# Unread products in TensorE's waits, pooling's copies and gates on ScalarE, and a third first tile four blocks behind

## The reference

```python
def _modulate(x, gain, shift, scale):
    return _rmsnorm(x, gain) * (1 + scale) + shift
...
def _pool_mixer(h, w_in, w_grp, scale, w_out):
    z = (h @ w_in).astype(jnp.float32).reshape(bsz, length, POOL_GROUPS, POOL_GROUP_DIM)
...
    pooled = (cs[:, hi, gidx] - cs[:, lo, gidx]) / cnt - z
    y = jnp.einsum('blgc,gcd->blgd', pooled, w_grp.astype(jnp.float32)).reshape(bsz, length, POOL_WIDTH)
    y = (y * scale.astype(jnp.float32)).astype(h.dtype)
    return y @ w_out
```

## Time and profile before

| | us |
|---|---|
| median of 3 runs | 1941.17 (1937.13 to 1942.27) |
| profiled execution, its time | 1939.76 |
| its span, first to last instruction | 1937.9 |
| PE busy | 1886.3 (97%) |
| DVE busy | 1535.0 (79%) |
| ACT busy | 920.9 (48%) |
| POOL busy | 400.0 (21%) |
| mean granted TensorE clock | 0.987 |

### The profile page before, as it was taken

The page is one execution under the profiler, slowest core; times in us unless marked ns, Lnnn a source line. Parts: engine busy times, 40 slices in busy tenths (PEclk is TensorE's granted clock), DMA queues, the critical chain, the costliest instruction groups (busy, mean ns, idle before and its releaser), DMA issues.

```text
span 1937.9 us, 38299 instructions
## 1 busy us (share of the span) xinstructions
PE 1886.3 (97%) x13216; PEld 1690.2 (87%) x13216; DVE 1535.0 (79%) x2617; ACT 920.9 (48%) x1476; POOL 400.0 (21%) x205
## 2 busy tenths in 40 slices
PE   5999999999999999999999899999999999999998
PEld 5999999999888888888888899999888888888887
DVE  6876589957998888888886669994889888886554
ACT  3464444544555544445444444454545544444544
POOL 1544468820000000000002347880000000000000
PEclk9999999999999999999998999999999999999999
DMA  8855345556655555578882345555664555555553
GB/s 319 321 198 195 132 164 180 182 181 207 211 168 173 174 173 173 173 268 318 323 309 95 118 147 173 180 176 183 217 209 160 173 174 173 173 173 187 193 194 130
DMA packets 104181, 376.42 MB, mean 194 GB/s; under 512 B 12464, under 2 KB 12464, under 8 KB 103856
## 3 DMA queue, kind: packets, MB, share of 16 engines
q1 hardware_dynamic: 103680, 373.43, 56.8%
q0 software_dynamic: 432, 2.10, 0.3%
HBM read 374.43 MB, written 1.05 MB: 194 GB/s over the span
## 4 chain that ended last, share of the span: by engine, by line
PE 55%; issue 19%; POOL 15%; DMA 4%; DVE 4%; ACT 2%; SPq 1%; POOLq 0%; DVEq 0%; ACTq 0%
PE O L1480 12%; PE O L1482 11%; PE O L1481 11%; POOL wL L405 9%; PE ring L1446 8%; POOL wL L392 6%; PE ring L1448 4%; DMA raw<-in_u 3%; PE ring L1232 2%; PE ring L1233 2%; PE ring L1234 2%; PE ring L1422 2%; DVE wL L673 2%; ACT wH L434 1%; PE O L1422 1%
## 5 line engine op out<-in xcount | busy, mean ns | idle before, releaser
L434 ACT ACTIVATE wH<-raw 128x1024 fp32r<-128x1024 f32 x608 | 644.8, 1061 | 921.6 <-DMA raw<-in_v 370.6
L673 DVE TENSOR_TENSOR wL<-raw,wH 128x1024 fp32r<-128x1024 f32 x416 | 509.2, 1224 | 234.8 <-ACT wH L434 229.9
L1232 PE MATMUL ring<-hX,wH 128*128 128x256 f32 x1512 | 434.5, 287 | 8.0 <-DVE wL L661 5.7
L1233 PE MATMUL ring<-hX,wH 128*128 128x256 f32 x1512 | 429.0, 284 | 0.0
L1234 PE MATMUL ring<-hX,wL 128*128 128x256 f32 x1512 | 428.8, 284 | 0.0
L1480 PE MATMUL O<-wH,gateH 128*128 128x512 f32 x1024 | 406.0, 396 | 0.3 <-DVE wL L673 0.3
L1482 PE MATMUL O<-wH,gateL 128*128 128x512 f32 x1024 | 400.2, 391 | 0.0
L1481 PE MATMUL O<-wL,gateH 128*128 128x512 f32 x1024 | 399.0, 390 | 0.0
L1446 PE MATMUL ring<-hX,wH 128*128 128x512 f32 x1024 | 367.3, 401 | 0.0
L1232 PEld LDWEIGHTS ring<-hX,wH 128*128 128x128 f32 x1512 | 291.2, 193 | 10.5 <-ACT UV L541 4.0
L1233 PEld LDWEIGHTS ring<-hX,wH 128*128 128x128 f32 x1512 | 291.3, 193 | 0.1
(11 more groups left out here) (171 smaller groups left out, 2174.0 us busy)
## 6 DMA issues: line engine op xcount, KB each, us to landing
raw<-in_u SPq DMA_DIRECT2D x256, 512.0 KB, 3.4
raw<-in_v SPq DMA_DIRECT2D x256, 512.0 KB, 3.5
ada_v<-in_ada SPq DMA_DIRECT2D x40, 512.0 KB, 4.8
raw<-in_w_in SPq DMA_DIRECT2D x32, 512.0 KB, 4.8
raw<-in_w_q SPq DMA_DIRECT2D x32, 512.0 KB, 3.5
ada_s<-in_ada SPq DMA_DIRECT2D x20, 512.0 KB, 5.3
ada_f<-in_ada SPq DMA_DIRECT2D x16, 512.0 KB, 10.7
raw<-in_w_out SPq DMA_DIRECT2D x16, 512.0 KB, 3.4
```

Source lines behind the costliest of these rows:

```text
L434: nc.scalar.activation(wH[s % RAW][:, :], raw[s % RAW][:, :], ACT.Copy).then_inc(s_h, 1)
L673: nc.vector.tensor_tensor(wL[s % RAW][:, :], raw[s % RAW][:, :], wH[s % RAW][:, :].bitcast(fp32), ALU.subtract).then_inc(s_low, 1)
L1232: mm(bank[:, 0:T], a, xH[:, k0 + k, :], start=(first and k == 0), stop=False)
L1233: mm(bank[:, 0:T], a, xL[:, k0 + k, :], start=False, stop=False)
```

## The change

It has six parts.

1. `keep_clock(n, bank)` puts n fp32 matmuls of 128 x 128 into PE's queue whose results nobody reads: 12, 11, 2 and 4 of them around the first norm's work, one behind each of the last four mixing tiles, 3 + 3 + 5 around the norms 1 and 3, 4 in front of the transposes that end layer 0, 3 + 5 around norm 2, 3 in front of the last spread. 70 in all.
2. `first_tiles` waits only for `hH` before the two products with it, takes the product with `hL` behind them, and runs the third tile four blocks behind the first two.
3. The modulations of 16 and 24 matmuls in `w_u` and `p_in` are taken in lots of eight between tiles.
4. The split of w_out's tile 3 on ACT and the low half of its tile 2 on DVE are issued a few operations earlier.
5. In the pool stage ACT copies the products into `Z` and rounds the scaled group product straight from PSUM to `gH`; DVE makes `gL` from PSUM; `UV` holds no full gates there. Two of the eight group results go into `ring` banks.
6. The sums of a pair of tiles are taken one pair later on DVE.

```diff
--- before.py
+++ after.py
@@ -256,7 +256,7 @@
         def pool_bank(n):
-            return O[n % 4]
+            return (O[0], O[1], O[2], O[3], ring[2], ring[3], O[0], O[1])[n]
@@ ACT, layer 0 @@
                     for f in range(10, SGU_FT):
+                        if f == 14:
+                            ahead(W_OUT, 0, 0)
                         gated_high(f, f + 1)
                     act.wait_ge(s_small, SMALL)
-                    warm_root()
                     for j in range(KT):
                         for kk in range(2):
-                            ahead(W_OUT, j // 2, 2 * (j % 2) + kk)
+                            if j or kk:
+                                ahead(W_OUT, j // 2, 2 * (j % 2) + kk)
+                            if j == 0 and kk:
+                                warm_root()
@@ ACT, layer 1 @@
+                    def pooled_high(n):
+
+                        act.wait_ge(s_pg, n + 1)
+                        f = POOL_ORDER[n]
+                        nc.scalar.activation(gH[:, n, :], pool_bank(n)[:, 0:T], ACT.Copy, scale=ps[:, f:f + 1])\
+                            .then_inc(s_gH, 1)
+
                     for j in range(KT):
                         ahead(base, j // 4, j % 4)
+                        act.wait_ge(s_pe, base + j + 1)
+                        nc.scalar.activation(Z[:, POOL_ORDER[j], PAD:PAD + T], ring[j % 4][:, 0:T], ACT.Copy)\
+                            .then_inc(s_bank_v, 1)
+                        if j > 5:
+                            pooled_high(2 * (j - 6))
+                            pooled_high(2 * (j - 6) + 1)
+                    for n in range(4, KT):
+                        pooled_high(n)
                     warm_root()
-                    for f in range(KT):
-                        gated_high(f, SGU_FT + f + 1)
@@ DVE, layer 0 @@
                     for f in range(12, SGU_FT):
+                        if f == 13:
+                            ahead(W_OUT, 0, 0)
                         gated_low(f)
@@ DVE, layer 1 @@
-                    def pooled_full(n):
-
-                        dve.wait_ge(s_pg, n + 1)
-                        nc.vector.tensor_scalar(UV[:, SGU_FT + n, :], pool_bank(n)[:, 0:T],
-                                                ps[:, POOL_ORDER[n]:POOL_ORDER[n] + 1], None, ALU.mult).then_inc(s_gf, 1)
-
                     def pooled_low(n):
+
                         dve.wait_ge(s_gH, SGU_FT + n + 1)
-                        nc.vector.tensor_tensor(gL[:, n, :], UV[:, SGU_FT + n, :], gH[:, n, :].bitcast(fp32),
-                                                ALU.subtract).then_inc(s_gL, 1)
...
+                        f = POOL_ORDER[n]
+                        nc.vector.scalar_tensor_tensor(gL[:, n, :], pool_bank(n)[:, 0:T], ps[:, f:f + 1],
+                                                       gH[:, n, :].bitcast(fp32), ALU.mult, ALU.subtract).then_inc(s_gL, 1)
...
-                        nc.vector.tensor_copy(Z[:, f, PAD:PAD + T], ring[j % 4][:, 0:T]).then_inc(s_bank_v, 1)
...
+                    for j in range(1, KT):
+                        ahead(base, j // 4, j % 4)
+                        if j == 4:
+                            modulations(7, (8, 9, 10), O[3], (3,))
+                        if j in (3, 5, 7):
+                            pool(j - 2)
+                    pooled_low(0)
+                    pooled_low(1)
+                    pool(KT - 1)
+                    for n in range(2, KT):
+                        pooled_low(n)
@@ PE, first_tiles @@
+                for k in range(KT):
+                    if k % 4 == 0:
+                        weights(k // 4, 2)
+                    pe.wait_ge(s_hH, KT * n + k + 1)
+                    for t in range(2):
+                        high(t, k)
+                    if count > 2 and k > 3:
+                        if k == 4:
+                            weights(0, 3)
+                        high(2, k - 4)
+                        low(2, k - 4)
                     pe.wait_ge(s_hin, KT * n + k + 1)
...
+                    for t in range(2):
+                        low(t, k)
+                if count > 2:
+                    weights(1, 3)
+                    for k in range(4, KT):
+                        high(2, k)
+                        low(2, k)
@@ PE @@
+            def keep_clock(n, bank=None):
+
+                for _ in range(n):
+                    mm((ring[3] if bank is None else bank)[:, 0:P], mean_w[:, :], ident[:, :], start=True, stop=True)
+
@@ PE, group_product @@
-                if n >= 4:
-                    pe.wait_ge(s_gf, SGU_FT + n - 3)
+                if n in (4, 5):
+                    pe.wait_ge(s_bank_v, 4 + KT + n + 3)
+                if n > 5:
+                    pe.wait_ge(s_gL, SGU_FT + n - 5)
@@ PE, start @@
             pe.wait_ge(s_const, 6)
+            pe.wait_ge(s_acc, 4)
+            keep_clock(12)
             modulations(acc_f, 0, 1, KT, O[3])
             for j in range(KT):
                 mean(0, j)
+            keep_clock(6)
+            pe.wait_ge(s_acc, ADA_FRONT - 3)
+            keep_clock(5)
             spread(0)
+            keep_clock(2)
             modulations(acc_f, 1, 2, ADA_FRONT, O[3][:, KT:])
+            keep_clock(4)
@@ PE, layer 0 @@
-                            modulations(acc_s, 0, 2, ADA_FRONT + 2 * KT, O[3])
+                            modulations(acc_s, 0, 1, ADA_FRONT + 2 * KT, O[3], signal=False)
                         if t == 10:
+                            modulations(acc_s, 1, 2, ADA_FRONT + 2 * KT, O[3][:, KT:])
...
+                    pe.wait_ge(s_bank_a, 4 + 16 + 14)
                     for f in range(12, SGU_FT):
                         mix_tile(f)
+                        keep_clock(1, ring[1])
@@ PE, layer 1 @@
-                        if j == 3:
-                            modulations(acc_v, 2, 5, ADA_U1, O[3])
-                        if j == 4:
+                        if j < 5:
+                            modulations(acc_v, j, j + 1, ADA_U1, O[3][:, KT * (j - 2):], signal=(j == 4))
+                        if j == 5:
                             pe.wait_ge(s_late, 48)
-                        if j > 3 and j % 2 == 0:
-                            group_product(j - 4)
-                            group_product(j - 3)
+                        if j in (5, 6):
+                            group_product(2 * (j - 5))
+                            group_product(2 * (j - 5) + 1)
@@ PE, second and fourth norm @@
                 mean(n, KT - 2)
+                keep_clock(3, ring[1])
                 mean(n, KT - 1)
+                keep_clock(3)
                 spread(n)
+                keep_clock(5)
@@ PE, end of a layer @@
                 if layer == 0:
                     pe.wait_ge(s_mod, 6)
+                    keep_clock(4, ring[3])
...
+                keep_clock(3)
                 spread(2 * layer + 2)
+                if layer == 0:
+                    keep_clock(5)
```

More of the change, by code:

```diff
@@ L869, in _ @@
                         for s in range(2):
-                            ahead(W_OUT, j // 2, 2 * (j % 2) + s)
+                            if j or s:
+                                ahead(W_OUT, j // 2, 2 * (j % 2) + s)
                             if 2 * j + s - 1 in ADA_W_OUT:
@@ L918, in _ @@
                         pooled = vtok[:, 0, 2 * g * T:(2 * g + 2) * T].rearrange("p (c t) -> p c t", c=2)
-                        after(steps[0])
                         after(step(nc.vector.tensor_tensor(pooled, lev[cur][:, :, PAD:PAD + T],
@@ L1237, in first_tiles, with high, low, weights @@
             def first_tiles(base, n, emptied, before, count):
+                def high(t, k):
+                    mm(ring[t][:, 0:T], wH[t][:, k * P:k * P + P], hH[:, k, :], start=(k == 0), stop=False)
+                    mm(ring[t][:, 0:T], wL[t][:, k * P:k * P + P], hH[:, k, :], start=False, stop=False)
+                def low(t, k):
+                    ins = mm(ring[t][:, 0:T], wH[t][:, k * P:k * P + P], hL[:, k, :], start=False, stop=(k == KT - 1))
+                    if k == KT - 1:
+                        ins.then_inc(s_pe, 1)
+                def weights(half, tiles):
+                    if n == 0:
+                        pe.wait_ge((s_first_l, s_first_r)[half], 2)
+                    else:
+                        pe.wait_ge((s_l0, s_l1)[half], base - HALVES[base >= BASE["p_in", 1]] + tiles)
                 for t in range(count):
@@ L1241, in first_tiles @@
                 for k in range(KT):
-                    if k % 4 == 0 and n == 0:
-                        pe.wait_ge((s_first_l, s_first_r)[k // 4], 2)
-                    elif k % 4 == 0:
-                        pe.wait_ge((s_l0, s_l1)[k // 4], base - HALVES[base >= BASE["p_in", 1]] + count)
-                    pe.wait_ge(s_hin, KT * n + k + 1)
-                    for t in range(count):
-                        a, b = wH[t][:, k * P:k * P + P], wL[t][:, k * P:k * P + P]
```

(15 more changed lines are left out.)

28 lines of the change are left out of this document (5 added, 23 removed).

## The result

| | before | after |
|---|---|---|
| median, range | 1941.17 us (1935.34 to 1943.88, 5 runs) | 1926.24 us (1922.91 to 1928.93, 5 runs) |
| span of the profiled execution | 1937.9 us | 1924.4 us |
| mean granted clock | 0.987 | 0.992 |

The ratio is 0.9923, 95% interval 0.9904 to 0.9941: the change is faster by 0.8%. The forecast was 1924.5.

The account below looks back on a forecast made before the run. TensorE, busy in nearly every slice, was taken as the bound, through idle stretches, lower clock and queued work. Terms summing to 16.7 us gave 1923.1 us for the profiled execution, 1924.5 for the median; range 1917 to 1932.

Parts of the forecast that it names:

- rival 3: Pool stage: ACT becomes the bound, its copies wait behind splits and the stage gains nothing; 1930 us, chance 0.06.
- rival 4: A later stage takes the gain back through loads or POOL's low halves; 4 us left, 1937 us, chance 0.04.
- rival 5: Slower: the filled waits are no waits, what PE awaits hangs on its own queue; 1955 us, chance 0.03.
- rival 1: The upper clock level holds in every filled wait; gain 24.0 us, 1917.2 us, chance 0.12.
- rival 2: Clock falls at all norms anyway, unread products run low, partly on the path; gain 10.5 us, 1930.7 us, chance 0.20.
- (A): Start of the kernel: high products begin earlier and the first 48 products end sooner; gain 3.0 us.
- (C): First w_out tile: DVE's low half begins earlier, the third tile's wait is filled, the clock holds; gain 2.5 us.
- (D): Second norm and w_q: earlier load chain and upper clock, less unread products on the path; gain 2.4 us.
- (F): Pool stage: work moved from DVE to ACT, UV wait and low clock gone; gain 5.5 us, the largest term.
- (E): End of layer 0 and third norm: unread products delay the transposes 0.6 us, clock rises earlier; gain 0.3 us.
- (G): Fourth norm: 1.4 us from the earlier load chain and 0.4 from the clock; gain 1.8 us.
- (B): Modulations in w_u split into two lots with full products between, so the clock does not fall; gain 1.6 us.

Follow-up runs that it names:

- the second execution: The unaltered changed kernel measured again on another chip, beside the follow-up runs, with its own profile: 1925.21 us, ratio 0.9927 to the kernel before.

## Why the prediction was right, and where it wasn't

The time was right to 1.7 us, and rivals 3, 4 and 5 fell. ACT is busy 12.4 of 30.2 us in the pool stage and none of PE's longer waits there is for it, the u and v stages gave back only 0.3, and the unread products alone gain. Rivals 1 and 2 were each right somewhere: the level held for the first tiles behind all three norms, but the means and unread products of the second and fourth still ran into a low stretch. But the sum was right because errors of both signs met: (A), (C), (D) and (F) came 5.9 us short of their forecasts, and (E), (G) and the rest with (H) 3.2 above. That part is luck. Between the two profiles 13.5 of the 16.7 us came; between the medians, 14.9.

- **(A), 3.0 forecast, 0.2 measured.** The step that failed is that the eleven unread products before the spread cost nothing. I had priced only the two behind it (up to 0.6), and my sum has no term for the eleven. They are 22 records at 0.215 us at the lower level, 4.7 us, and DVE had inv at 29.2: 2.4 us late. The clock was up from 15.1 to 18.5 and then fell during the single columns. With five products (A) is 2.1. Where the means end earlier (the second execution) the spread comes at 29.15, and (A) is 2.25 with all eleven. The first stage also never became faster than DVE: 9.23 of 9.50 us busy, with products ending near 44 and not 41. And there a low half of DVE (34.94) stood beside POOL's subtraction (34.85) and took 1.73 us, 0.69 in the kernel before, so that PE waited 1.12 for hX.
- **(B)** right to a tenth, by 26 products in 2.9 us at 1.00, and by the experiment with the modulations whole.
- **(C), 2.5 against 1.7.** The clock part came (24 products in 2.9 us at 1.00). DVE began the low half at 153.36, with all before it shifted by 1.8 only 0.2 earlier instead of 1.0, because the moved split on ACT brought POOL's subtraction forward too, to 151.19, beside DVE's gate, which took 1.10 us instead of 0.42. The wait of 1.76 us was filled, but 0.61 of it was left.
- **(D), (G), 2.4 and 1.8 against 1.9 and 3.4.** Both norms run alike now: 3.4 us are won behind the first product, of which 0.8 to 0.9 is the order (1.4 forecast) and 2.5 the level (2.0 in D, only 0.4 in G). Ahead of it (D) pays 1.5 for the unread products at the lower level, twice the 0.7 forecast, and (G) nothing on balance (7.6 us as before); the kernel before had run its spread there at the lower level too. In the second execution, with the level up, the same piece of (G) takes 6.6.
- **(E), 0.3 against 1.0.** The transposes lost 1.4 us and not 0.6, and not by the unread products: those are over by 1021.1, and PE still waits 0.54 for `otok`. PE's last product came 5.1 us earlier than before (1019.61 for 1024.67), but ACT, with its split behind a load and then its table load, got to the copy only 3.5 us earlier (1020.52 for 1024.06). Against that the level held for all 72 products of the first tiles.
- **(F), 5.5 against 3.7.** The mechanism was right and the size of DVE's part was off. PE's own work was 27.2 us, as forecast (27.4). The term that was mis-sized is the waits: I had added 0.7, for the last pair's sums alone, at 0.7 us for every sum. That pair cost 0.87. But PE also waited 0.92 and 1.22 for the two pairs before it, for which the sum has nothing, because DVE's sums take up to 1.8 us instead of 0.7 beside POOL. Together that is 3.0. Without POOL's subtractions the stage took 27.6, with the last wait alone. The kernel before had the same long sums; its mean of 1.3 us for the four of 540 columns could have been read there.

Of the signs that I had named, the UV wait is gone, the fall at 123 is gone, and the wait behind w_q's tile 3 is 0.7. The stage of 27 to 29 us (30.2), the third w_out tile without a wait (0.61) and the end of the first 48 products at 38.5, 41 or 43 (near 44) did not come.

## What to carry to other kernels

Filling TensorE's waits keeps its clock only at a small profit, and every filler must be priced at the lower clock, where it costs nearly twice (0.44 us instead of 0.24 here), and against the moment at which the awaited value is ready, not against the end of the old wait. Work moved between two engines changes more than their busy times: look at which operations run beside each other before and after. Where the clock falls at another norm in each execution, forecast and judge the sum, and compare places only with a second profile.

## What the runs showed of the hardware

- In these traces an operation of DVE with both inputs in SBUF takes longer when a subtraction on POOL is under way: 1.10 us instead of 0.42 for 256 columns, 1.80 instead of 0.71 for 540; the one that reads PSUM stayed at 0.48. In each of four cases (1.73, 1.10, 1.80 and 1.65 us) it ended 0.3 to 0.6 us behind the end of POOL's, as if it had waited for it, and where DVE began first it was POOL that took longer (1.70). The Trainium skill, "SBUF — State Buffer", section "Who interferes with whom", says just this: a DVE instruction with two SBUF inputs contends with a GpSimd instruction that reads SBUF, not with one that only writes it. The trace agrees, and so does the run in which POOL mostly writes (memsets of 0.51 us, all sums at 0.7). By that rule DVE's moved gates, which read PSUM, should be free of it, and the sums not. None of the gates ran beside POOL in this trace, so only the sums show it.
- The level fell with PE counted as busy: 4.05 us of products of one column in one piece were followed by 6.8 us at 0.50, and two lots of 1.84 with 24 full products between by no fall. 20.4 us went by at 0.50 with PE busy for 16.4.
- The same program falls in different places: low at the fourth norm in one execution and not in the other.
